# Prompt attention of a hybrid decoder step: scores as two fp32r products, one output bank per branch, transposes two jobs behind the scores

## The reference, cut to what matters

```python
s = einsum('btgrd,bngd->bgrtn', qf, kc[:, :, 0]) * ATT_SCALE      # 63 compressed keys
p = masked_softmax(s, cmask);  o_cmp = einsum('bgrtn,bngd->btgrd', p, kc[:, :, 1])
sc = einsum('btgrd,bgtkd->bgrtk', qi, kvg[..., 0, :]) * ATT_SCALE # selected: N_SEL=16 blocks of 64
s = einsum('bctgrd,bckgd->bcgrtk', qblk, band[:, :, :, 0]) * ATT_SCALE  # window of 512
o_b = gates[..., 0:1] * o_cmp + gates[..., 1:2] * o_sel + gates[..., 2:3] * o_win
```

## Time and profile before

| | us |
|---|---|
| median of 3 runs | 3207.34 (3193.57 to 3207.39) |
| the profiled execution | 3209.55 |
| its span, first to last instruction | 3207.8 |
| PE busy in the span | 3034.9 (95%) |
| DVE busy | 1075.8 (34%) |
| ACT busy | 588.9 (18%) |
| POOL busy | 1084.0 (34%) |

### The profile page before, as it was taken

One profiled execution on the slowest core, in us unless ns is written; L12 is line 12 of the kernel. 1 busy time (PEld: TensorE's weight loads), 2 busy tenths in 40 slices (PEclk: granted clock), 3 DMA queues, 4 the chain that ended last, 5 costly groups with the idle time before them and its releaser, 6 DMA issues.

```text
span 3207.8 us, 46542 instructions
## 1 busy us (share of the span) xinstructions
PE 3034.9 (95%) x20048; PEld 2809.8 (88%) x20048; DVE 1075.8 (34%) x1475; ACT 588.9 (18%) x932; POOL 1084.0 (34%) x598
## 2 busy tenths in 40 slices
PE   7999889989999769999999999999999999999996
PEld 5999868877777528899999999989898999999996
DVE  5000363345555121332222222334525222322223
ACT  3100014545444120111110000121112000011112
POOL 6432132410000162433333333433444333333331
PEclk9999988989999789999999999999999999999998
DMA  3211322310000352111111111031021111111111
GB/s 126 74 48 60 126 68 79 135 53 1 1 1 1 100 158 85 40 47 47 46 46 46 46 46 46 26 130 43 27 93 46 47 46 46 46 46 46 46 39 53
DMA packets 197871, 184.76 MB, mean 58 GB/s; under 512 B 7301, under 2 KB 181634, under 8 KB 196394
## 3 DMA queue, kind: packets, MB, share of 16 engines
q1 hardware_dynamic: 187498, 149.25, 14.7%
q0 software_dynamic: 10240, 33.56, 3.4%
HBM read 161.88 MB, written 25.09 MB: 58 GB/s over the span
## 4 chain that ended last, share of the span: by engine, by line
PE 80%; issue 7%; DVE 6%; POOL 3%; ACT 2%; DMA 1%; another core or an unknown queue 1%; SPq 0%; POOLq 0%; ACTq 0%; DVEq 0%
PE psum L259 47%; PE psum L390 6%; PE psum L283 5%; PE psum L1295 4%; PE psum L1565 3%; PE psum L1621 3%; PE psum L1599 2%; PE psum L271 1%; POOL whl L229 1%; DVE ntmp L358 1%; PE psum L1955 1%; POOL srows L950 1%; PE psum L1279 1%; PE psum L305 1%
## 5 line engine op out<-in xcount | busy, mean ns | idle before, releaser
L259 PE MATMUL psum<-xhi,whl 128*128 128x344 f32 x4704 | 875.0, 321 | 4.5 <-issue 2.3
L229 POOL TENSOR_TENSOR whl<-wraw,zeroc 128x1024 fp32r<-128x1024 f32 x186 | 353.6, 1901 | 1266.2 <-PE psum L259 872.8
L259 PEld LDWEIGHTS psum<-xhi,whl 128*128 128x128 f32 x4704 | 765.8, 188 | 5.4 <-issue 4.5
L259 PE MATMUL psum<-xlo,whl 128*128 128x344 f32 x2352 | 500.4, 321 | 0.0
L232 POOL TENSOR_TENSOR whl<-wraw,whl 128x1024 fp32r<-128x1024 f32 x186 | 451.8, 2429 | 14.6
L259 PE MATMUL psum<-ahi,whl 128*128 128x344 f32 x2304 | 427.5, 320 | 0.0
L259 PEld LDWEIGHTS psum<-xlo,whl 128*128 128x128 f32 x2352 | 399.3, 189 | 0.0
L259 PEld LDWEIGHTS psum<-ahi,whl 128*128 128x128 f32 x2304 | 373.1, 188 | 3.0 <-DVE hT L450 2.5
L441 DVE CAST ahi<-frel 128x1032 fp32r<-128x1032 f32 x64 | 178.3, 2786 | 520.1 <-ACT frel L434 520.1
L450 DVE TENSOR_TENSOR hT<-hT,psum 128x1032 f32<-128x1032 f32 x128 | 157.3, 1229 | 489.1 <-PE psum L259 426.9
L432 ACT ACTIVATE frel<-psum 128x1032 f32<-128x1032 f32 x64 | 66.1, 1034 | 1206.3 <-PE psum L259 1188.6
(11 more groups left out here) (361 smaller groups left out, 3401.8 us busy)
## 6 DMA issues: line engine op xcount, KB each, us to landing
wraw<-in_w_ffn SPq DMA_DIRECT2D x128, 512.0 KB, 3.8
wraw<-in_w_in_ab SPq DMA_DIRECT2D x26, 512.0 KB, 3.6
h_spill<-hT SPq DMA_DIRECT2D x2, 4128.0 KB, 12.5
hT<-h_spill SPq DMA_DIRECT2D x8, 1032.0 KB, 8.0
wraw<-in_w_in_c SPq DMA_DIRECT2D x16, 512.0 KB, 3.9
xtok<-in_x_prompt SPq DMA_DIRECT2D x2, 2048.0 KB, 13.0
wrow<-in_state_win_kv SPq DMA_DIRECT2D x4, 1024.0 KB, 13.9
wraw<-in_w_out_ab SPq DMA_DIRECT2D x8, 512.0 KB, 4.0
```

Source lines behind the costliest of these rows:

```text
L229: pool.tensor_tensor(whl[:, s, 0, :], raw, zeroc[:, 0:1].to_broadcast([P, UNIT]), ALU.add).then_inc(w_hi, 1)
L259: last = pe.matmul(psum[:, 3 * bset + c, 0:TC], w, rhs[ah][:, k0 + k, c * TC:(c + 1) * TC], start=(k == 0 and n == 0), stop=(k == kn - 1 a ...
```

## The change

The fp32 product of the scores is replaced by two fp32r products. For each query tile and head ACT writes q rounded to fp32r (the high part) and DVE the rest (the low part) into the two halves of the partitions of `qhl` (`act_queries`, `dve_queries`), one tile ahead, in the middle of the s jobs of the tile before. The keys stand in both halves of the partitions, as high part `kh` (ACT) and low part `kl` (DVE, `dve_keys_low`); the zero halves and `pool_zeros` go. The product of `qhl` with `kh` and that with `kl` add up to all four products of parts.

The jobs of a tile are now eight s and then eight w. Step n issues the scores of job n, the transposes of n-2 and the values of n-3. The transposes use banks 4 and 5 in turn, four blocks each, and ACT alone evacuates them. The values of the eight heads of a branch go side by side into one bank (6 or 7, by the group of branch and tile), and DVE combines a branch once for each tile, with five instructions, instead of once for each job with three. `qhl` lies where `srows` lies, so the gather of sample 0 now waits for the last combine, as only that of sample 1 did.

```diff
-        kte = at("kte", R_G, [P, 4, SEQ])
-        kto = at("kto", R_W + 16384, [P, 4, SEQ])
+        kh = at("kh", R_G, [P, 4, SEQ], F32R)
+        kl = at("kl", R_W + 16384, [P, 4, SEQ], F32R)
...
+        qhl = at("qhl", R_W, [P, 2, HB, P], F32R)
...
-        psm = at("psm", R_H + 26784, [P, 4])
-        wgt = at("wgt", R_H + 26816, [P, 4])
+        psm = at("psm", R_H + 26784, [P, 2, HB])
+        wgt = at("wgt", R_H + 26848, [P, 2, HB])
+        otmp = at("otmp", R_H + 26912, [P, 512])
...
         for i in range(NT):
-            body = [("c", i, 0)] + [(x, i, h) for h in range(HB) for x in "sw"]
+            body = [("c", i, 0)] + [(x, i, h) for x in "sw" for h in range(HB)]
             if i:
                 body.insert(3, ("t", i - 1, 0))
             jobs += body
-        jobs += [None, None, ("t", NT - 1, 0)]
+        jobs += [None, None, None, ("t", NT - 1, 0)]
...
-                act.activation(kte[0:64, bg, c], psum[0:64, 5 + n % 2, :], ACT.Copy).then_inc(p_kd, 1)
-                act.activation(kto[64:P, bg, c], psum[64:P, 5 + n % 2, :], ACT.Copy).then_inc(p_kd, 1)
+                act.activation(kh[:, bg, c], psum[:, 5 + n % 2, :], ACT.Copy).then_inc(p_kd, 1)
...
+        def dve_keys_low(dve):
+            for n in range(8):
+                bg, half = n // 2, n % 2
+                dve.wait_ge(p_kd, n + 1)
+                c = slice(512 * half, 512 * half + 512)
+                dve.tensor_tensor(kl[:, bg, c], psum[:, 5 + n % 2, :], kh[:, bg, c].bitcast(F32), ALU.subtract)\
+                    .then_inc(p_kl, 1)
...
+        def act_queries(act, i):
+            if i >= 2:
+                act.wait_ge(p_qk, soft_no[job_no[("w", i - 2, HB - 1)]] + 1)
+            for q, high, low in query_parts(i):
+                act.activation(high, q, ACT.Copy).then_inc(p_qh, 1)
+
+        def dve_queries(dve, i):
+            dve.wait_ge(p_qh, 2 * i + 2)
+            for q, high, low in query_parts(i):
+                dve.tensor_tensor(low, q, high.bitcast(F32), ALU.subtract).then_inc(p_ql, 1)
+
...
-            pe.wait_ge(p_kd, 16)
-            pe.wait_ge(p_z, 2)
+            pe.wait_ge(p_kl, 8)
             pe.wait_ge(m_cm, 2)
...
+                if kind == "s" and h == 0:
+                    pe.wait_ge(p_ql, 2 * i + 2)
...
-                    last = pe.matmul(psum[:, bank, 0:w], qB[:, h // 2, qs],
-                                     (kte, kto)[h % 2][:, bg, (lo + b0) * P:(lo + b0) * P + w],
-                                     start=True, stop=True)
+                    cols = slice((lo + b0) * P, (lo + b0) * P + w)
+                    pe.matmul(psum[:, bank, 0:w], qhl[:, i % 2, h, :], kh[:, bg, cols], start=True, stop=False)
+                    last = pe.matmul(psum[:, bank, 0:w], qhl[:, i % 2, h, :], kl[:, bg, cols], start=False, stop=True)
...
                 if kind == "t":
-                    pe.wait_ge(p_cb, soft_no[last_soft(i)] + 1)
+                    pe.wait_ge(p_cb, group(("w", i)) + 1)
                 else:
                     pe.wait_ge(p_p, soft_no[n] + 1)
...
+                for b0 in range(0, blocks(jobs[n]), 4):
+                    u = first_bank[n] + b0 // 4
+                    if u == 0:
+                        pe.wait_ge(m_oe, 2 * (NB + 1))
+                    if u == 1:
+                        pe.wait_ge(p_kl, 8)
+                    if u >= 2:
+                        pe.wait_ge(p_ea, u - 1)
+                        if u - 2 in tail_banks:
+                            pe.wait_ge(p_tl, tail_banks[u - 2] + 1)
+                    for b in range(b0, min(b0 + 4, blocks(jobs[n]))):
+                        o = psum[:, 4 + u % 2, (b - b0) * P:(b - b0 + 1) * P]
...
+                    last.then_inc(p_T, 1)
...
+                pe.wait_ge(p_ea, banks_done(n))
+                gq = group(jobs[n])
+                if h == 0 and gq >= 2:
+                    pe.wait_ge(p_cb, gq - 1)
+                bank = 6 + gq % 2
...
-                        last = pe.matmul(psum[:, bank, 0:64], ptb[:, k % 2, b * P:(b + 1) * P],
+                        last = pe.matmul(psum[:, bank, 64 * h:64 * h + 64], ptb[:, k % 2, b * P:(b + 1) * P],
                                          kvp[:, lo + b, c0:c0 + 64], start=(b == 0), stop=(b == nb - 1))
...
-            for n in range(len(jobs) + 2):
+            for n in range(len(jobs) + 3):
                 if n in soft_no:
                     scores(n)
-                if n - 1 in work_no:
-                    transposes(n - 1)
-                if n - 2 in soft_no:
-                    values(n - 2)
...
+                if n - 2 in first_bank:
+                    transposes(n - 2)
+                if n - 3 in soft_no:
+                    values(n - 3)
...
                 if k >= 2:
-                    act.wait_ge(p_T, work_no[SOFT[k - 2]] + 1)
-                if k >= 4:
-                    act.wait_ge(p_wt, k - 3)
+                    act.wait_ge(p_T, banks_done(SOFT[k - 2]))
+                x = "sw".index(kind)
+                if h == 0 and i >= 1:
+                    act.wait_ge(p_cb, group((kind, i - 1)) + 1)
                 s = psum[:, 2 * (k % 2):2 * (k % 2) + 2, :].rearrange("p a b -> p (a b)")[:, 0:w]
                 act.activation(pbuf[:, k % 2, 0:w], s, ACT.Exp, bias=nmax[:, k % 4:k % 4 + 1],
-                               accum_out=psm[:, k % 4:k % 4 + 1]).then_inc(p_p, 1)
+                               accum_out=psm[:, x, h:h + 1]).then_inc(p_p, 1)
...
+                for b0 in range(0, blocks(jobs[n]), 4):
+                    u = first_bank[n] + b0 // 4
+                    act.wait_ge(p_T, u + 1)
+                    w = min(4, blocks(jobs[n]) - b0) * P
+                    act.activation(ptb[0:m, k % 2, b0 * P:b0 * P + w], psum[0:m, 4 + u % 2, 0:w], ACT.Copy)\
+                        .then_inc(p_ea, 1)
+
+            act_queries(act, 0)
+            for n in range(len(jobs) + 3):
                 if n in soft_no:
                     softmax(n)
-                if n - 1 in work_no:
-                    evacuate(n - 1)
+                    if jobs[n][0] == "s" and jobs[n][2] == 4 and jobs[n][1] + 1 < NT:
+                        act_queries(act, jobs[n][1] + 1)
+                if n - 2 in first_bank:
+                    evacuate(n - 2)
...
+                x = "sw".index(kind)
+                s, v = link("dve", dve.reciprocal(wgt[:, x, :], psm[:, x, :]))
...
+                g = gates[:, i, :].rearrange("p (h x) -> p h x", x=3)[:, :, 1 + x]
+                s, v = link("dve", dve.tensor_tensor(wgt[:, x, :], wgt[:, x, :], g, ALU.mult))
+                dve.wait_ge(s, v)
                 dve.wait_ge(p_pv, k + 1)
-                dve.wait_ge(p_cb, k)
-                o = out[:, 64 * h:64 * h + 64]
-                dve.scalar_tensor_tensor(o, psum[:, 6 + k % 2, 0:64], wgt[:, c:c + 1], o, ALU.mult, ALU.add)\
...
+                dve.wait_ge(p_cb, gq)
+                s, v = link("dve", dve.tensor_tensor(otmp[:, :].rearrange("p (h d) -> p h d", h=HB),
+                                                     psum[:, 6 + gq % 2, :].rearrange("p (h d) -> p h d", h=HB),
+                                                     wgt[:, x, :].unsqueeze(2).to_broadcast([P, HB, 64]), ALU.mult))
+                dve.wait_ge(s, v)
+                dve.tensor_tensor(out, out, otmp[:, :], ALU.add).then_inc(p_cb, 1)
+
+            dve_queries(dve, 0)
+            for n in range(len(jobs) + 3):
                 if n in soft_no:
                     maxima(n)
-                if n - 1 in work_no:
-                    evacuate(n - 1)
-                if n - 2 in soft_no:
-                    combine(n - 2)
+                    if jobs[n][0] == "s" and jobs[n][2] == 5 and jobs[n][1] + 1 < NT:
+                        dve_queries(dve, jobs[n][1] + 1)
+                if n - 2 in first_bank and jobs[n - 2][0] == "t":
+                    low_half(n - 2)
+                if n - 3 in soft_no and (jobs[n - 3][0] == "c" or jobs[n - 3][2] == HB - 1):
+                    combine(n - 3)
...
             for b in range(NB):
-                if b == 0:
-                    pool.wait_ge(m_T, GROUPS_BEFORE[NB + 1])
                 if b >= 2:
                     pool.wait_ge(sP, PE_S[f"sk{b - 2}_3"])
                     pool.wait_ge(s_vh, b - 1)
-                if b == 1:
-                    pool.wait_ge(p_cb, len(SOFT))
+                if b == 0:
+                    pool.wait_ge(p_cb, GROUPS)
                 gather(pool, cache_sel[0], srows[:, b % 2, :, :], b, range(NT), s_sr[b % 2])
```

141 lines of the change are left out of this document (52 added, 89 removed).

## The result

The changed kernel takes 3215.35 us (median of 20 runs, 3204.04 to 3251.83) against 3206.51 (20 runs, 3193.57 to 3210.28) for the kernel before: a ratio of 1.0037 [1.0021, 1.0053] over the runs (the two medians alone give 1.0028). The forecast of 3158, its range of 3128 to 3188 and all the faster cases are missed. The runs of the changed kernel spread over 48 us, those of before over 17. The profiled execution took 3204.83 (span 3203.0) and is one of its fastest; before's took 3209.55.

A forecast was written before the change was run, and what follows sets the result against it. PE's own work was taken to bound the late tiles, work plus waits the early ones. 85.3 + 171.9 + 48 + 4 + 6 + 8 = 323 us against 373.5, with -2 and +2: -50, so 3158 us, range 3128 to 3188.

The forecast's parts named there:

- all the faster cases: Forecast (chance 0.57), PE setting every tile (3132 us, 0.17), slow early clock (3185, 0.10), weight loads in the open (3178, 0.07).
- Scores, 55 us: Prompt attention scores: two fp32r products instead of one fp32 product save 55 us of PE work, bounds 0 and 65.
- The rival of loads in the open: Scores: each of 384 records carries an exposed weight load of at least 0.055 us; saving 29, 3178 us, chance 0.07.
- Steady jobs: Score jobs within tiles: 85.3 us in the first four tiles, 171.9 in the last four, where PE sets them.
- The locked steps: Rival: evacuation of a job must end before the next scores start; 75 us slower, 3282 us, chance 0.04.
- The failed step: ACT query copies and DVE subtractions amid the s jobs, plus DVE's combines: 8 us together, of 0 to 25.
- a clock that stays at half in the second and third tile: Rival: less PE work leaves early tiles at half clock; saving 22, 3185 us, chance 0.10.
- The rest of a tile, 6 us: The `c` and `t` jobs of each query tile keep their instructions: 6 us a tile, 48 in all.
- Start and end: Start gains 2 us (0 to 4.7) from fewer key copies; end loses 2 (0 to 5.6) from the later gather.
- 85.3 + 24 + 6: First four tiles: 85.3 us of jobs, 6 a tile for `c` and `t`, 6 for the first `c` at half clock.

The follow-up runs named there:

- the last filled kernel: Changed kernel plus idle bf16 products on PE at the start, in the first three tiles and ahead of s2 and s5: 3214.51 us, 1.0003 times before.

## Why the prediction was wrong

**Scores, 55 us: right in kind, 10 to 15% too large.** In the chain the first record of a job takes 0.28 to 0.29, each further one 0.23. A 512-column product at a job's start is 0.52 instead of 0.454, a second one 0.46, and a 128-column pair 0.22 as forecast. With 0.05 more for each of 128 jobs the saving is about 48. The pair of the last tile is 6.25 in the old order (3.67 + 2.5 = 6.2 in the new one), forecast 6.0, before 7.36. The rival of loads in the open is refuted by the 512-column records, 0.23 each where it needed 0.28. (The 128-column records, 0.11 each, don't decide it: 0.055 for the columns and 0.055 for a load is what the rival itself was priced from.) The Trainium skill's rule (TensorE: Matmul & The Clock Gate, The mechanism) is that a load overlaps products under way only where its row group differs; these rows don't agree, since every record has its own load into all rows and still takes 0.23.

**Steady jobs: right.** At full clock a job of the fourth tile takes 1.88 to 1.90 (1.82 forecast), of the second 1.16 to 1.26 (1.15), of five blocks 2.51 to 2.60 (2.38 and 2.42), of eight 3.50 to 3.67 (3.58). The locked steps (2.78 in the fourth tile) didn't happen.

**The failed step: "PE still has the scores of the next job to do, so this costs between 0 and 1.2 for each of seven tiles", with 8 us for copies and combines.** The bound holds only where PE also has a values product at that step. I had the list of jobs and did not look which step the copies fall on: it is the one behind `t`, which has none. There the wait is 2.0 to 2.5 us in six tiles, of which 1.1 to 1.2 in the late tiles stay when the copies are gone (the step had no cover even for ACT's ordinary work, a wait that the forecast put at nothing). In five of the six the clock falls behind it, and the loss is the 15 us of stage, or 27 by the ratios, between the changed kernel and the one with its queries on POOL. With the copies at this step the ratio is 1.0037, without them 0.9952: this step decides the sign.

**Clock, the wrong kind of rival.** I gave 0.10 to a clock that stays at half in the second and third tile, with a price of 28 us, and set it at 1.0 in the forecast. Of that, the second tile happened (0.74, 34.6 us for 16 x 1.15 + 6 = 24.4 forecast) and the third in part (0.91, 37.2 for 29.8 by the same sum). What no case held is that waits in the late tiles can cost again at half speed: tiles 5 to 8 are at 0.92 to 0.97 and take 233.0 with the drain, forecast 200, and PE is busy for 92 to 94% of them where I had over 95. The Trainium skill (TensorE: Matmul & The Clock Gate, A second HAM failure mode: psum-queue depth-cycling) describes a kernel in which short pauses between groups of matmuls keep the clock moving between its two levels, and says that the price is in throughput. This trace agrees: a clock of 0.69 over 937 to 945 us, and nine stretches at half speed in the stage.

**The rest of a tile, 6 us: too small.** The steps around `c` and `t` cost 9 to 10 in the fourth and fifth tile (39.8 less 16 x 1.89, 50.1 less 8 x 5.11). About 2.5 of it is the wait of the failed step, which leaves some 7. That one engine now evacuates both banks of `c` is a part of this: the run with the old scores has the wait for it (1.19 us) by itself. Its +15 us of stage are those of the whole new order, and how much of them is `c` isn't shown. "The `c` and `t` jobs keep their instructions" was true of PE and false of ACT.

**Start and end.** +2.2 us at the end is the forecast in its size, but not shown to be the gather's: the same stretch takes 2155.5 to 2168.3 us in the other runs with the late gather, and 2162.8 in the one with the early gather. The first transposes of the window rows come 3.2 us later, inside the 0 to 5 of the forecast, yet PE waits there for DVE's `ptc` (0.32 us, as before), not for the rows. The gain of 2 at the start can't be read: two profiles of the same changed kernel begin the stage at 668.0 and 676.4 us.

**Where the sum went.** By the forecast the first four tiles take 85.3 + 24 + 6 = 115 and took 140.4; the last four with the drain 200 and took 233.0; 8 us were set aside for the copies. 25 + 33 - 8 = 50, the whole of the forecast gain. Of these 50 the copies are 15 by the POOL run. Its own stage, 358.2, is 43 above the forecast without the 8: tile by tile 1, 9, 3, 11, 4, 4, 5 and 7 us, so most in the second (clock 0.75) and the fourth (0.81). The two runs of the old order show that the thin tiles would have given nothing in any order tried without filler (138 and 144 us for 136 before).

**The median against the profile.** The stages of the two profiled executions are equal, and the medians differ by 9 us. The profiled execution of the changed kernel had a clock of 0.961 over its span; its runs at 3238.76 and 3251.83 us had 0.948, its median runs 0.958. Span times clock lies between 3063 and 3081 in all 20 runs (0.6%), the span between 3202 and 3250 (1.5%), so most of the spread goes with the clock. Which tiles are slow in the long runs isn't shown, since only short ones were profiled. In the other variants the difference of the profiled stage and that of the ratios from before agree within about 5 us (8 for the last filled kernel); for the changed kernel they are 0 and +12, in its repetition 0 and +17. Its profiled executions are among its fastest, so the ratios, and not the equal stages, tell what it usually loses.

**Left open.** Why the old order with copies on ACT kept a better clock in the second and third tile than with copies on POOL (.78 and 1.00 for .65 and .87) isn't settled. Neither is why 1.19 us of waiting was followed by half speed in one place and 1.21 by full speed in another. A version of the old order in which the fp32r products are kept and the early tiles are shortened on ACT and DVE wasn't tried.

## What to carry to other kernels

Before work is put on an engine "in the middle", write down for that very step what each engine still has in hand; a step with a missing product (behind a `t` here) is the worst place for it, and two jobs further the same copies were 21 us cheaper. Price a wait of PE as the wait plus the half-speed work that can follow it (here in five of six), and expect a cut of PE's work to pay only where PE was the bound: here -24 us in four full tiles and +2 in four thin ones. Where a change has two parts, time each alone: the new scores without the new order beat both kernels (0.9922).
